# VectorE takes the w_ada units in loading order; the test matmuls at the end are taken out

## The reference, cut to what matters

```
c_act = jax.nn.silu(c)
ada = (c_act @ w_ada + b_ada)[:, None, :]            # w_ada: 2048 x 12288
sh1, sc1, gt1, sh2, sc2, gt2 = jnp.split(ada, 6, axis=-1)
h  = _rms(x, g_norm1) * (1 + sc1) + sh1              # start of the second block
x  = x + gt1 * (merged @ w_out)
h2 = _rms(x, g_norm2) * (1 + sc2) + sh2
gate, up = jnp.split(h2 @ w_ffn_in, 2, axis=-1)
x  = x + gt2 * ((jax.nn.silu(gate) * up) @ w_ffn_out)
```

## Time and profile before

| | us |
|---|---|
| median of 3 runs | 2777.35 (2776.05 to 2779.42) |
| profiled execution | 2776.69 |
| its span, first to last instruction | 2774.9 |
| TensorE busy (matmuls, ends modelled) | 2646.6 |
| VectorE busy | 1743.9 |
| ScalarE busy | 1179.8 |
| DMA | 582.37 MB, mean 210 GB/s |

### The profile page before, as it was taken

The page is one execution under the profiler, slowest core; times in us unless marked ns, Lnnn a source line. Parts: engine busy times, 40 slices in busy tenths (PEclk is TensorE's granted clock), DMA queues, the critical chain, the costliest instruction groups (busy, mean ns, idle before and its releaser), DMA issues.

```text
span 2774.9 us, 29598 instructions
## 1 busy us (share of the span) xinstructions
PE 2646.6 (95%) x11925; PEld 2169.9 (78%) x11925; DVE 1743.9 (63%) x2157; ACT 1179.8 (43%) x1465; POOL 25.5 (1%) x25
## 2 busy tenths in 40 slices
PE   9999999998888888888999999999998999999999
PEld 8888888776776676677788888888777778888888
DVE  6787787666666666666656555456666665555554
ACT  6444444333333333333566454444443343344443
POOL 0000000000000000000001000000000000000000
PEclk9999999999999999999999999999999999999999
DMA  8555556665556665566555444555556655555554
GB/s 314 196 199 227 210 200 230 251 246 227 227 231 253 243 236 225 233 247 241 198 180 182 152 160 160 196 185 179 182 197 238 240 219 197 193 187 196 184 196 137
DMA packets 82631, 582.37 MB, mean 210 GB/s; under 512 B 9408, under 2 KB 9792, under 8 KB 12608
## 3 DMA queue, kind: packets, MB, share of 16 engines
q1 hardware_dynamic: 82352, 580.38, 56.5%
q10 hardware_dynamic: 144, 0.12, 0.0%
HBM read 578.36 MB, written 2.10 MB: 209 GB/s over the span
## 4 chain that ended last, share of the span: by engine, by line
PE 61%; DVE 19%; DMA 13%; ACT 4%; issue 2%; POOL 0%; ACTq 0%; SPq 0%; DVEq 0%
PE bank L837 19%; PE bank L839 19%; PE bank L838 19%; DMA raw<-in_w_gu_dram 10%; DVE wlo L1274 8%; DVE adacc L1701 7%; DMA raw<-in_w_down_dram 3%; ACT whi L882 3%; PE bank L556 2%; PE bank L636 1%; DVE aL L1431 1%; ACT aH L957 1%; DVE tmp L1422 1%; DVE tmp L1412 1%; PE bank L674 0%
## 5 line engine op out<-in xcount | busy, mean ns | idle before, releaser
L1274 DVE TENSOR_TENSOR wlo<-raw,whi 128x1024 fp32r<-128x1024 f32 x886 | 1076.8, 1222 | 939.4 <-ACT whi L882 937.2
L882 ACT CAST whi<-raw 128x1024 fp32r<-128x1024 f32 x886 | 917.4, 1051 | 1260.5 <-PE bank L839 591.6
L837 PE MATMUL bank<-whi,hH 128*128 128x512 f32 x2528 | 1016.5, 402 | 88.8 <-DVE wlo L1274 88.1
L838 PE MATMUL bank<-wlo,hH 128*128 128x512 f32 x2528 | 996.4, 394 | 0.0
L839 PE MATMUL bank<-whi,hL 128*128 128x512 f32 x2528 | 996.0, 394 | 0.0
L837 PEld LDWEIGHTS bank<-whi,hH 128*128 128x128 f32 x2528 | 481.4, 190 | 211.3 <-DVE wlo L1274 113.5
L839 PEld LDWEIGHTS bank<-whi,hL 128*128 128x128 f32 x2528 | 480.9, 190 | 103.0
L838 PEld LDWEIGHTS bank<-wlo,hH 128*128 128x128 f32 x2528 | 482.1, 191 | 95.8
L837 PE MATMUL bank<-whi,aH 128*128 128x512 f32 x704 | 278.8, 396 | 26.8 <-DVE wlo L1274 26.8
L838 PE MATMUL bank<-wlo,aH 128*128 128x512 f32 x704 | 276.5, 393 | 0.0
L839 PE MATMUL bank<-whi,aL 128*128 128x512 f32 x704 | 276.4, 393 | 0.0
(11 more groups left out here) (302 smaller groups left out, 1426.0 us busy)
## 6 DMA issues: line engine op xcount, KB each, us to landing
raw<-in_w_gu_dram SPq DMA_DIRECT2D x176, 1024.0 KB, 4.9
raw<-in_w_ada_dram SPq DMA_DIRECT2D x96, 1024.0 KB, 8.6
raw<-in_w_down_dram SPq DMA_DIRECT2D x88, 1024.0 KB, 4.8
raw<-in_w_in_dram SPq DMA_DIRECT2D x62, 1024.0 KB, 5.1
raw<-in_w_in2b_dram SPq DMA_DIRECT2D x56, 1024.0 KB, 4.8
raw<-in_w_out_dram SPq DMA_DIRECT2D x32, 1024.0 KB, 4.8
raw<-in_w_in2a_dram SPq DMA_DIRECT2D x8, 1024.0 KB, 4.9
raw<-in_w_mla_dram SPq DMA_DIRECT2D x8, 1024.0 KB, 4.8
```

The lines of the kernel that those rows point to most:

```text
L837: e.matmul(o, xh[:, kt, sl], wh[:, i, :], start=k == 0, stop=False)
L838: e.matmul(o, xh[:, kt, sl], wl[:, i, :], start=False, stop=False)
L882: e.copy(whi[i][:, :, :], raw[u % RAW][:, 2 * hf:2 * hf + 2, :]).then_inc(*ev("act_hi", c, 0))
L1274: e.tensor_tensor(wlo[i][:, :, :], raw[u % RAW][:, 2 * hf:2 * hf + 2, :], f(whi[i][:, :, :]), ALU.subtract).then_inc(*ev("dve_lo", c, 0))
```

## The change

In the planner the base slot of a w_ada unit is taken from the visit that brings in the last chunk of the unit ahead (plus one, the slot in which VectorE subtracts it), where it was the visit of that chunk. In VectorE's program `ada_tiles` comes ahead of `side_work`, where it came behind it. Sums, products and the first slot of the last gates follow the base. The matmuls of `forms`, their operand and the wait for it are gone.

```diff
-            s = self.vis[self.last_chunk[u], 0]
+            s = self.split_at[self.last_chunk[u]] + 1
             self.ada_base[v] = s
...
-            if i == 0:
-                ones_b = at("ones_b", [P, 2 * P], BF16, o)
...
-            forms(e)
-
-        def forms(e):
-
-            e.wait_ge(*on("dve_ones", "last"))
-            many = ones_r[:, :].unsqueeze(1).to_broadcast([P, 4, P])
-            for n, (o, st, mv) in enumerate((
...
-                for _ in range(5):
-                    e.matmul(o, st, mv, start=True, stop=True)
...
-                if s == len(pl.visits) - 8:
-                    e.memset(ones_b[:, :], 1.0).then_inc(*ev("dve_ones", "last"))
...
+                ada_tiles(s)
                 side_work(s)
-                ada_tiles(s)
                 ada_sums(s)
```

More of the change, by code:

```diff
@@ L19 @@
 F32R = mybir.dt.float32r
-BF16 = mybir.dt.bfloat16
 I32 = mybir.dt.int32
```

## The result

The changed kernel takes 2611.49 us (2611.35 to 2612.39, 4 runs) against 2778.19 for the kernel before in the same comparison: a ratio of 0.9401, 95% interval 0.9385 to 0.9418. The forecast was 2601, its range 2590 to 2670. The profiled execution took 2611.4 us, its span is 2609.6.

A forecast was written before the change was run, and what follows sets the result against it. The prediction took the raw ring's round in the dense w_ada stages, closed by adacc's releases, as the bound; 175.0 + 1.5 = 176.5 us off the profiled 2776.69 gave 2600.2, as a median 2601, range 2590 to 2670.

The forecast's parts named there:

- The bound: Dense w_ada stages: TensorE waits 147.8 us for wlo, as the raw ring closes a round of 13.38 us.
- The slot: Both feed-forwards: with w_ada's base two slots earlier TensorE sets the pace; 140.7 and 34.3, together 175.0 us less.
- VectorE's cost at nothing: Feed-forward rounds: VectorE, 79% busy at the new pace, is fast enough; nothing added.
- Its upper bound of 67 us: Three of a round's four subtractions each wait out a cast: 67 us given back, 2668 us, chance 0.12.
- The added wait: VectorE stops for a w_ada unit's landing two slots earlier; the unit lands in time, cost nothing.
- The rule against it: Weight loads: fixed DMA part paid by each load alone makes 13.2 us a round, nothing won; sum kept.
- the estimate of 4.4 us: One 1 MB load: about 2.0 us fixed plus bytes at 436 GB/s, set near the trace's 4.79.
- Loads one at a time: Raw ring: each load leaves only when the one before landed; 72 us more, 2848 us, chance 0.04.
- The stages with one unit in four: Stages with one w_ada unit in four weight units: nothing waits for a weight, nothing won there.
- What else moves along: Group transposition and reduction, L715 products, last gates' broadcasts come two slots earlier; nothing, else some 2.3 us at four places.
- The test products: 25 matmuls on L862 at the kernel's end: without them the end is SyncE's, 1.5 us less.

The follow-up runs named there:

- One slot later: The changed kernel with the base of the w_ada units one slot later still; 2625.8 us, ratio 0.9449.
- the order alone: The kernel before with adacc steps moved ahead of the block tasks in a slot, base slot as before, test products gone; 2737.44 us, ratio 0.985.
- VectorE at 97% and 98% busy: The changed kernel with three adacc steps in four issued twice; 2630.26 us, ratio 0.9467.

## Why the prediction was right, and where it was not

*The bound.* Right. The loss belonged to the dense w_ada stages and was a closed loop through the raw ring; with the loop cut below TensorE's pace, the waits for wlo are gone and the clock is 1.00.

*The slot.* Right, and sized: 175.0 us were forecast, 172.5 came. The rounds went to 11.08 us in the first feed-forward, where 11.06 and 10.96 had been taken. One slot later, single rounds take the computed 11.2, and with the order alone a round without a block task takes 12.37 where 12.38 stood, so the links were added up rightly.

*VectorE's cost at nothing.* Right for the feed-forwards. Its upper bound of 67 us rested on three of four subtractions waiting out a cast; with VectorE at 97% and 98% busy, 4.0 us of the feed-forwards show.

*The added wait.* Right at nothing: 6.8 us before 360 steps, before and after.

*The rule against it.* From 600 to 665 us a w_ada unit lands 5.2 us after its issue in the median, where it was 8.7 in a burst, and a unit of gate and up 5.4. Each load does pay its own time. The round doesn't grow, for the loads overlap: 287 GB/s. Two readings in the prediction are off and changed nothing. The 4.79 us of the earlier trace rows is the first load of a burst and not a load on its own, but over the whole changed kernel the w_ada units, which leave alone, take 4.8 in the median. And the estimate of 4.4 us beside it is for GpSimd's path, as the heading that it names says, while these loads leave on SyncE's queue; the sum used nothing of it. Loads one at a time, the slower rival, would have made the round 14.37.

*The stages with one unit in four.* Here the step failed: "nothing waits for a weight now, and nothing is won there". I asked there only what the change could win, and priced no loss: VectorE's 80.88%, beside a TensorE that didn't wait, seemed to leave room for one. The share says nothing about which task TensorE stands waiting for. Two units of w_ada moved ahead of the gating, and its distance to the transposition was short already: 1.9 us of stops behind that task were in the table of waits of the kernel before. That row, with four steps of 0.75 us moved ahead of it, would have given two stops of some 4 us (0.95 and 3.0); 3.7 came. The term is +8.8 us, 8.25 of it these two stops and their slow clock, which holding back two units takes away again. That the forecast still came within 0.5% is owed to the size of the other terms, not to this one.

*What else moves along.* Better than costed: the stops behind L715 are gone in the changed kernel. The prediction read them as four stops of 9.1 us in all; they were two, which that row counts once for the weight load and once for the matmul:

```profile
PEld bank L715 <- DVE late_part L1714: 5.0, 2, 2.9
...
PE bank L715 <- DVE late_part L1714: 4.1, 2, 2.5
```

The earlier slot doesn't cause them, then; one slot later they show again (6.2 us in two).

*The test products.* 1.5 us forecast, 1.5 measured.

## What to carry to other kernels

Where a ring of buffers is filled in order, the consumer that releases late holds up every load behind it: add up the round from one release to the next, link by link, and compare it with the pace of the engine that should set it. Moving a release forward by the work that can go behind it is worth a round's difference times the number of rounds, and nothing beyond that pace. And when work is moved forward on an in-order engine, list each task it overtakes and look in the table of waits for which of them another engine already stands waiting: there the move cost most here (8.25 us). A task without such a row can cost too: the sum of the keys had none, and got two stops of 0.6 us.

## What the runs showed of the hardware

VectorE at 97% busy over 398 us (260.00 and 126.08 us of the first two stages above) cost TensorE nothing, with four buffers between them; over the next 223 us, at 98%, TensorE stood still for 1.3 us. Two stops of at most 3.7 us each were followed by a slow clock (0.50 and then 0.72 over 2 us stretches behind the first), which cost some 2.8 us in all on top of the 5.4 us by which the stops grew. In the kernel before, TensorE stood idle for 0.5 us at the same place, and the clock stayed at 1.00 (206 to 222 us). With the order alone it stood idle for 2.0 us at each of the two places; behind the first the clock fell to 0.50 (214 to 216 us), behind the second it stayed at 1.00 (414 to 424 us).
